# A product-key expert layer: six gathers of 128 rows split into 120 and 8

## The reference, cut to what matters

```python
eidx = jnp.take_along_axis(cand_idx, pos, axis=-1)      # 8 heads x 16 experts per token
g = jax.nn.softmax(top_s, axis=-1)
u = expert_down[eidx]
a = jax.nn.gelu(jnp.einsum('cd,chkd->chk', xc, u).astype(jnp.float32), approximate=False)
vv = expert_up[eidx]
y = jnp.einsum('chk,chkd->cd', (g * a).astype(vv.dtype), vv)
```

## Time and profile before

| | |
|---|---|
| median of 3 runs | 906.3 us |
| lowest and highest run | 903.89 and 907.79 us |
| the profiled execution's own time | 904.22 us |
| its span, first to last instruction | 902.4 us |
| mean granted clock of TensorE | 0.985 of full speed |
| PE, DVE, ACT, POOL busy | 88%, 62%, 48%, 27% of the span |
| read from HBM | 311.01 MB, of which the gathers 268.45 MB |

### The profile page before, as it was taken

How to read it: one execution, slowest core, us unless ns; L and a number is a source line. 1 busy time by engine, 2 the same in 40 slices (tenths; PEclk the granted TensorE clock), 3 DMA queues, 4 the chain that set the end, 5 groups by cost and what they waited for, 6 DMA issues and landing times.

```text
span 902.4 us, 10121 instructions
## 1 busy us (share of the span) xinstructions
PE 796.0 (88%) x3195; PEld 450.2 (50%) x3195; DVE 561.9 (62%) x1396; ACT 433.6 (48%) x1078; POOL 242.8 (27%) x268
## 2 busy tenths in 40 slices
PE   7999999999999999889898997989787877788776
PEld 7999987785455455444343552444232222222221
DVE  5555344123778767777776748787676766666443
ACT  5435555333245554667444445535355353535333
POOL 0000000000143333433343341624333333343310
PEclk9999999999999999999999899999999999999999
DMA  9898532072399999999999999999999999999993
GB/s 332 235 293 288 195 133 94 1 280 93 142 405 421 391 423 421 415 422 421 422 420 421 421 421 410 401 416 423 421 422 421 422 422 421 422 422 421 422 420 133
DMA packets 63317, 314.24 MB, mean 348 GB/s; under 512 B 7899, under 2 KB 12068, under 8 KB 30500
## 3 DMA queue, kind: packets, MB, share of 16 engines
q0 software_dynamic: 36864, 268.45, 71.9%
q1 hardware_dynamic: 25308, 43.61, 13.8%
q10 hardware_dynamic: 1096, 1.59, 1.2%
HBM read 311.01 MB, written 2.62 MB: 348 GB/s over the span
## 4 chain that ended last, share of the span: by engine, by line
PE 42%; DMA 38%; ACT 9%; issue 5%; DVE 5%; POOL 1%; POOLq 0%; ACTq 0%
DMA weights<-in_expert_rows,expert_idx 24%; PE y L1480 10%; DMA qkvb<-in_expert_rows,expert_idx 7%; PE v_bank L1480 7%; DMA mem_k<-in_expert_rows,expert_idx 6%; PE v_bank L1235 4%; PE a_bank L1245 4%; PE h_psum L1235 4%; PE v_bank L1245 3%; PE a_bank L1235 3%; PE h_psum L1245 3%; ACT diag L779 1%; ACT L770 1%; ACT L762 1%; ACT spare_r L676 1%
## 5 line engine op out<-in xcount | busy, mean ns | idle before, releaser
L597 POOL DMA_INDIRECT weights<-in_expert_rows,expert_idx x172 | 161.4, 939 | 260.7 <-PE y L1480 118.1
L770 ACT ACTIVATE gelu<-dots,stat 128x1 f32<-128x1 f32 x256 | 75.3, 294 | 307.0 <-DVE dots L1169 300.6
L1480 PE MATMUL v_bank<-weights,diag 128*128 128x512 f32 x344 | 169.9, 623 | 39.8 <-ACT diag L779 39.8
L1480 PE MATMUL y<-weights,diag 128*128 128x512 f32 x344 | 161.7, 606 | 17.7 <-ACT diag L779 17.5
L1169 DVE CUSTOM_DVE_ANT_0 weights<-a_bank,weights 128x1024 f32<-128x1024 f32 x86 | 105.3, 1224 | 74.9 <-DMA weights<-in_expert_rows,expert_idx 74.8
L1169 DVE CUSTOM_DVE_ANT_0 weights<-h_psum,weights 128x1024 f32<-128x1024 f32 x86 | 105.1, 1223 | 54.7 <-DMA weights<-in_expert_rows,expert_idx 52.6
L597 POOL DMA_INDIRECT qkvb<-in_expert_rows,expert_idx x54 | 51.0, 944 | 316.6 <-DVE expert_idx L1026 234.6
L1480 PEld LDWEIGHTS v_bank<-weights,diag 128*128 128x128 f32 x344 | 61.1, 193 | 144.7 <-ACT diag L779 94.0
L1480 PEld LDWEIGHTS y<-weights,diag 128*128 128x128 f32 x344 | 62.4, 191 | 98.2 <-issue 56.9
L779 ACT ACTIVATE diag<-ident,wgt 128x128 f32<-128x128 f32 x256 | 102.8, 402 | 8.4
L774 ACT ACTIVATE wgt<-gelu,gates 128x1 f32<-128x1 f32 x256 | 75.4, 295 | 8.3
(11 more groups left out here) (288 smaller groups left out, 1281.7 us busy)
## 6 DMA issues: line engine op xcount, KB each, us to landing
weights<-in_w_in SPq DMA_DIRECT2D x5, 2048.0 KB, 32.3
weights<-in_w_xk SPq DMA_DIRECT2D x2, 2048.0 KB, 16.6
weights<-in_w_xv SPq DMA_DIRECT2D x2, 2048.0 KB, 10.7
weights<-in_w_out SPq DMA_DIRECT2D x2, 2048.0 KB, 8.8
weights<-in_w_xq SPq DMA_DIRECT2D x2, 2048.0 KB, 7.9
weights<-in_w_xo SPq DMA_DIRECT2D x2, 2048.0 KB, 11.1
weights<-in_expert_rows,expert_idx POOLq DMA_INDIRECT x172
weights<-in_w_in SPq DMA_DIRECT2D x2, 1024.0 KB, 8.5
```

The source lines that it names most:

```text
L597: pool.indirect_dma_start(ROWS[buffer(n)], None, expert_rows, bass.IndirectOffsetOnAxis(ap=IDX[:, H % 3, k:k + 1], axis=0))\
L770: nc.scalar.activation(gel[:, i:i + 1], dots[:, i:i + 1], ACT.Gelu, scale=rms("root_p", n // SPT)).then_inc(gelu_done, 1)
L1480: ins = nc.tensor.matmul(YP[t][:, b * BLK:(b + 1) * BLK], diag[:, i, :], ROWS[r][:, D + b * BLK:D + (b + 1) * BLK], start=False, stop=last)
```

## The change

Six slots of the second tile, 136, 160, 184, 208, 232 and 248, are gathered in two parts. The first takes the rows of partitions 0 to 119 with the indices where they are. The second takes the rows of partitions 120 to 127, with indices that lie on partitions 0 to 7 of a new small tile `few_idx`, a column for each of the six slots. SP fills that column by a transfer of 8 words out of `IDX` when the head's indices are ready; POOL waits for it (`ld_few`, a semaphore for each) between the two gathers. SP's first such transfer stands ahead of the output of tile 0 in its list, the other five between the outputs of tile 0 and tile 1. Both gathers count on the same `row_in`, and `landed(n)` gives the count that the dot waits for.

```diff
+IN_TWO = (136, 160, 184, 208, 232, 248)
+MOST = 120
...
+    def landed(n):
+
+        return 16 * sum(2 if m in IN_TWO else 1 for m in users(n) + [n])
...
+        few_idx = sb("few_idx", [P - MOST, len(IN_TWO)], i32)
...
+        ld_few = [sem(f"ld_few{j}") for j in range(len(IN_TWO))]
...
+            def few(j):
+
+                H, k = IN_TWO[j] // PK, IN_TWO[j] % PK
+                sp.wait_ge(idx_ready, H + 2)
+                sp.dma_start(few_idx[:, j:j + 1], IDX[MOST:P, H % 3, k:k + 1]).then_inc(ld_few[j], 16)
+
+            few(0)
             for t in range(T):
+                if t == 1:
+                    for j in range(1, len(IN_TWO)):
+                        few(j)
                 sp.wait_ge(out_ready, t + 1)
...
-                pool.indirect_dma_start(ROWS[buffer(n)], None, expert_rows,
-                                        bass.IndirectOffsetOnAxis(ap=IDX[:, H % 3, k:k + 1], axis=0))\
-                    .then_inc(row_in[buffer(n)], 16)
+                if n in IN_TWO:
+                    j = IN_TWO.index(n)
+                    pool.indirect_dma_start(ROWS[buffer(n)][0:MOST, :], None, expert_rows,
+                                            bass.IndirectOffsetOnAxis(ap=IDX[0:MOST, H % 3, k:k + 1], axis=0))\
+                        .then_inc(row_in[buffer(n)], 16)
+                    pool.wait_ge(ld_few[j], 16)
+                    pool.indirect_dma_start(ROWS[buffer(n)][MOST:P, :], None, expert_rows,
+                                            bass.IndirectOffsetOnAxis(ap=few_idx[:, j:j + 1], axis=0))\
+                        .then_inc(row_in[buffer(n)], 16)
+                else:
+                    pool.indirect_dma_start(ROWS[buffer(n)], None, expert_rows,
+                                            bass.IndirectOffsetOnAxis(ap=IDX[:, H % 3, k:k + 1], axis=0))\
+                        .then_inc(row_in[buffer(n)], 16)
...
-                dve.wait_ge(row_in[buffer(n)], 16 * (len(users(n)) + 1))
+                dve.wait_ge(row_in[buffer(n)], landed(n))
```

## The result

| | before | after |
|---|---|---|
| median | 905.49 us (4 runs, 903.89 to 907.79) | 952.19 us (4 runs, 951.44 to 956.64) |
| span of the profiled execution | 902.4 us | 950.3 us |
| ratio after to before | | 1.0522, 95% interval 1.05 to 1.0544 |

The change costs 46.7 us, 7.8 us for each of its six slots. The forecast was 904.1 us, the range ended at 912.5 us, and rival A, the costliest, ended at +11.7 us.

The account below looks back on a forecast made before the run. The prediction took the full DMA engines, with one late engine, as the bound. Terms of -2.3 us for moved rows and +0.1 us for completion, the rest 0, took 906.3 to 904.1 us; range 901.2 to 912.5 us.

Parts of the forecast that it names:

- rival A: Six slots' gathers: two engines sharing one path into SBUF make them slower, +4.3 to +11.7 us, 914.3 us; chance 0.2.
- What bounds the kernel: Second tile's steady part: full DMA engines bound it at 422 GB/s, and every slot waits for one late engine.
- Rows moved from one gather to two: Six slots' gathers: leaving the late engine out relieves it, -3.2 to -1.3 us, taken as -2.3 us.
- Rival B: Six slots' gathers: the late engine isn't the one left out, no gain, 906.3 to 908.2 us; chance 0.22.
- My forecast: Gathers and final drain: some net relief of the late engine, -3.2 to -1.3 us, median 904.1 us; chance 0.42.
- rival C: Drain at the end: all engines become level, -6.2 us, 900.1 us; chance 0.13.
- Six more gathers on POOL: POOL's issue: 1.24 us per extra gather fits into 1.56 us of idle time before each; term 0.
- small transfers: SP's six index transfers and POOL's wait: about 4 us from issue to landing, nothing on the path; term 0.
- completion: Six slots complete two gathers each, and the dot waits for both on one semaphore: +0.1 us.

Follow-up runs that it names:

- e6: Changed kernel, but the six slots gather only the 64 rows of partitions 32 to 95, the other 64 left out: 898.96 us, ratio 0.9919.
- e11: Changed kernel's 120 and 8 rows, but in six slots in a row, 209 to 214: 929.53 us, ratio 1.0274.
- e2: Changed kernel without the second gather, so only 120 rows in the six slots: 948.15 us, ratio 1.0444.
- e3: Changed kernel, but 128 rows in one gather and 8 rows more into a free tile in the six slots: 912.87 us, ratio 1.0055.
- e1: Changed kernel with small transfers and POOL's waits kept, but 128 rows gathered at once in the six slots: 907.99 us, ratio 1.0008.
- e8: Changed kernel with the six slots gathered in 124 and 4 rows: 981.72 us, ratio 1.0841.

## Why the prediction was wrong

*What bounds the kernel* held (the highest rate of a slice is 423 GB/s in the earlier trace rows, not 426): the transfers are the bound, and one engine is last. Fewer rows in e6 gave back 7.0 us for 7.4 us of transfer, and slower rows in e11 cost 24.7.

*Rows moved from one gather to two* is the step that failed. It counted rows per engine, "8 x 0.31 = 2.49 us ahead" for the one left out and 0.31 us for an extra row, and took the 0.31 us itself for granted. The row that gave it, 422 GB/s at share 1.01, is of gathers of 128 rows. In e11's gathers of 120 and 8 rows a row takes about twice as long (203 GB/s); of the other shapes tried only e6's 64 rows keep the rate. The sign of the term was wrong: not -2.3 us but +40.7 for the 120 rows (e2) and +5.4 for the 8 (e3).

*Rival A* had the mechanism, with the words "two engines may write into the same part of SBUF while another part rests", and the DMA port swizzle of the Trainium skill's "SBUF — State Buffer" beside it. It was given 0.2, and its price was too low by a factor of four: at most +11.7 us, from 2.49 us a slot and a relief from the lag, where 46.7 us, 7.8 a slot, was measured. The 2.49 is confirmed as the price of the two-part rows alone, 2.7 us a slot in e11. Missing was what a slot costs beyond that: 7.8 - 2.7 = 5.1 us for a single one, in e11 8.6 us once for six. The drain divides the 5.1: most engines lost 5.7 us a slot, 3 more than the 2.7, and the late one 2 more again. The likely reason of the 3 is the border. Engines are several us apart, as the earlier trace rows shows. Those ahead are in the odd gather while the others still write their own rows of the gathers before, and the other way round when it ends; so slots 158 and 159 suffered too, and 203 rows moved at half rate for 128. I used the spread of the engines as an argument against A ("the engines drift several us against each other already without any loss of rate"). Read this way it was one for it: in gathers of 128 each engine writes a path of its own and may drift freely, and just this drift makes a foreign row expensive. That the surplus isn't paid by each slot is shown by e11 against the change; that the border is its cause is argued, and why the late engine loses more than the others stays open.

*Rival B* came true beside it. The late engine was not relieved: alone for 14 us at the end where it was 3.2, and 8.0 us a slot lost where most lost 5.7. My forecast and rival C both rested on moving work away from it. Which engine each gather leaves out no view shows, so whether a relief was there and was eaten stays open.

*Six more gathers on POOL*, *small transfers* and *completion*: 0, 0 and +0.1 us. e1 bounds the middle one at -0.1 to +0.25% (907.99 against 907.45 us). POOL's list shows 1.20 us for the second gather, inside the idle time, as worked out. At slot 208, the closest, POOL did not wait for its indices in the changed kernel either. No run measures the 0.1 us of *completion* by itself.

*The range*: A's upper end, 906.3 + 11.7 = 918.0 us, was made of one doubling of 8 rows, and the range cut it at 912.5; neither could hold a cost for which I had no term. "No row shows a gather of another shape" was written down and should have widened the range upward, since full engines have no reserve.

## What to carry to other kernels

When the DMA engines are full, keep every gather at 128 partitions: of the other shapes tried here all but one, the 64 rows of partitions 32 to 95, slowed the stream, from 0.9 us a slot for 8 rows more to 12.6 us for 124 and 4 rows, and the change slowed the rows around it as well. Before splitting a transfer, ask which engine then writes which partitions, not only how many rows each has. And read the rate beside the DMA share: at a share of 1.0 the rate was anything from 147 to 422 GB/s.

## What the runs showed of the hardware

- Two sets of 64 partitions, 32 to 95 and 0 to 63, with the same number of rows: 898.96 and 924.36 us.
- A slot in 120 + 8, 112 + 16 or 124 + 4 rows cost 7.8, 5.6 and 12.6 us more in a stream of gathers of 128.
- The share of the DMA engines doesn't fall when the rate halves: 1.00 to 1.03 at 201 to 205 GB/s (e11).
- With 124 and 4 rows eight of the sixteen engines ran dry: a share of 0.50 to 0.53 at 206 to 221 GB/s (e8).
- Late dots leave PE idle, and the granted clock falls after it: PE is idle from 656 to 658 us in the changed kernel, and from 664 to 666 us the granted clock is 0.50, the lower of its two levels (1.2 of 2.4 GHz). The DMA share stays at about 1.0 meanwhile, so this looks like a consequence rather than a further cost; it wasn't tried.
